# The head of a two-layer decoder step reordered, and the rounding of activations and weights taken in turn with scale and shift

## What is computed

```python
mod = silu(c) @ w_ada[layer] + b_ada[layer]            # 6 x 1024: shift, scale, gate, twice
h = rms_norm(x, norm1) * (1 + sc1) + sh1
y = even_mixer(h, ...)    # layer 0: one input projection (3592 columns), DeltaNet and short convolution
    # layer 1: q, k, v projection (3072 columns), dilated window attention
x = x + g1 * (y @ w_out)
h = rms_norm(x, norm2) * (1 + sc2) + sh2
x = x + g2 * hier_moe(h)  # 32 experts, the two best of the best group for each token
```

## Time and profile before

| | us |
|---|---|
| median of 3 runs | 1290.17 (1289.33 to 1292.78) |
| the profiled execution | 1288.16 |
| its span, first to last instruction | 1286.3 |
| PE busy | 1169.5 (91%) |
| DVE busy | 491.4 (38%) |
| ACT busy | 318.6 (25%) |
| POOL busy | 41.9 (3%) |

### The profile page before, as it was taken

How to read it: one execution, slowest core, us unless ns; L and a number is a source line. 1 busy time by engine, 2 the same in 40 slices (tenths; PEclk the granted TensorE clock), 3 DMA queues, 4 the chain that set the end, 5 groups by cost and what they waited for, 6 DMA issues and landing times.

```text
span 1286.3 us, 18265 instructions
## 1 busy us (share of the span) xinstructions
PE 1169.5 (91%) x7640; PEld 794.1 (62%) x7640; DVE 491.4 (38%) x1228; ACT 318.6 (25%) x600; POOL 41.9 (3%) x85
## 2 busy tenths in 40 slices
PE   3879999989788899999999699998897999999996
PEld 2679878778555655555553599865466455555444
DVE  0267233452323423333333533355425233333334
ACT  0266301020101221111111444454413211111114
POOL 0000000200010000000000200200001000000000
PEclk9679999997779899999999799999997999999998
DMA  9643122396646199999998344599881799999851
GB/s 287 210 141 110 55 66 66 115 336 212 205 153 259 47 402 386 378 380 373 374 377 272 114 135 155 173 319 330 270 343 34 283 419 366 375 363 385 355 202 43
DMA packets 122886, 317.21 MB, mean 247 GB/s; under 512 B 9136, under 2 KB 93136, under 8 KB 96166
## 3 DMA queue, kind: packets, MB, share of 16 engines
q1 hardware_dynamic: 115652, 304.87, 64.3%
q0 software_dynamic: 2336, 7.84, 2.0%
q10 hardware_dynamic: 4802, 3.18, 1.0%
HBM read 309.37 MB, written 6.49 MB: 246 GB/s over the span
## 4 chain that ended last, share of the span: by engine, by line
PE 81%; DVE 12%; ACT 3%; issue 2%; DMA 1%; SPq 1%; ACTq 0%; DVEq 0%
PE bank L1544 17%; PE bank L1105 11%; PE bank L1565 9%; PE bank L1507 5%; PE bank L1582 4%; PE bank L1069 3%; PE bank L1168 3%; PE bank L1071 3%; PE bank L1070 3%; PE bank L1202 3%; PE bank L1160 2%; DVE arena L2001 2%; DVE xT L2007 2%; PE bank L1064 1%; PE bank L1525 1%
## 5 line engine op out<-in xcount | busy, mean ns | idle before, releaser
L1544 PE MATMUL bank<-arena 128*64 128x512 f32 x768 | 225.2, 592 | 0.5 <-DVE gslot L2455 0.5
L1544 PEld LDWEIGHTS bank<-arena 128*64 128x64 f32 x768 | 71.7, 137 | 108.7 <-issue 108.0
L1707 ACT ACTIVATE arena<-bank 128x512 f32<-128x512 f32 (+7 forms) x150 | 76.5, 536 | 206.3 <-PE bank L1071 54.2
L1565 PE MATMUL bank<-ring,scratch 128*64 128x512 f32 x512 | 120.3, 613 | 1.1 <-ACT scratch L1707 1.1
L1544 PE MATMUL bank<-ring,arena 128*64 128x512 f32 x256 | 112.5, 592 | 0.0
L1069 PE MATMUL bank<-hTh,wh 128*128 128x320 f32 x304 | 96.7, 318 | 14.3 <-DVE wl L2066 14.3
L1105 PE MATMUL bank<-hT,ring 128*128 128x320 f32 x352 | 99.6, 440 | 0.6 <-issue 0.6
L1070 PE MATMUL bank<-hTl,wh 128*128 128x320 f32 x304 | 96.1, 316 | 0.0
L1071 PE MATMUL bank<-hTh,wl 128*128 128x320 f32 x304 | 96.0, 316 | 0.0
L2007 DVE SCALAR_TENSOR_TENSOR xT<-bank,mod,xT 128x256 f32<-128x256 f32 x144 | 69.0, 479 | 66.2 <-PE bank L1105 55.7
L2007 DVE SCALAR_TENSOR_TENSOR scratch<-scratch,gslot,bank 128x256 f32<-128x256 f32 x32 | 21.7, 678 | 163.3 <-ACT scratch L1917 163.3
(11 more groups left out here) (309 smaller groups left out, 1746.1 us busy)
## 6 DMA issues: line engine op xcount, KB each, us to landing
ring<-in_w_exp_down_dram SPq DMA_DIRECT2D x64, 1024.0 KB, 8.9
arena<-in_w_exp_gate_dram SPq DMA_DIRECT2D x48, 1024.0 KB, 8.8
arena<-in_w_exp_up_dram SPq DMA_DIRECT2D x48, 1024.0 KB, 10.8
ring<-in_w_ada_dram SPq DMA_DIRECT2D x44, 1024.0 KB, 11.7
ring<-in_w_exp_gate_dram SPq DMA_DIRECT2D x16, 1024.0 KB, 10.8
ring<-in_w_exp_up_dram SPq DMA_DIRECT2D x16, 1024.0 KB, 10.2
ring<-in_w_in_even_dram SPq DMA_DIRECT2D x14, 1024.0 KB, 5.6
ring<-in_w_qkv_odd_dram SPq DMA_DIRECT2D x8, 1024.0 KB, 5.6
```

The source lines that it names most:

```text
L1544: ins = pe.matmul(bank[0][SLOTS * w:SLOTS * w + SLOTS, :].rearrange("p (w f) -> p w f", w=2), hg[:, q % 2, c, s0:s0 + SLOTS], weights[w][: ...
L1565: ins = pe.matmul(bank[2 + d][rows, :], hidT[:, P * f + SLOTS * w:P * f + SLOTS * w + SLOTS], x[:, w, D * f + 512 * d:D * f + 512 * d + 51 ...
L1707: return act.activation(dst, src, ACT.Copy)
```

## The change

In the head the squares go right behind x, DVE adds them up (as it already did for the norms behind the mixers), and PE sums only the last chunk over the partitions. The row of u = 6 and turn 4 stand ahead of the spread. The two weight halves that layer 0 needs first are rounded ahead of hp; ACT then does four hp, and after that one hh and one hp in turn; the third half comes last. In layer 1 half 0 goes ahead of hp, half 1 behind the third hh, half 2 last. DVE follows the same order. POOL multiplies by the token's factor first in layer 0's first norm (into another buffer, `tiny`), by the gain first in the other norms. PE no longer waits in `norm` for hp and hs. The halves 0 to 2 leave the mixers' lists.

```diff
@@ plan_head @@
                     for c in range(C):
                         fills("head", ("x", c), ("dve", ("x", c)))
                         makes("head", "dve", ("x", c))
+                        if c >= 2:
+                            makes("head", "dve", ("acc", "01", c - 1))
+                    makes("head", "dve", ("acc", "01", C - 1))
+                    makes("head", "act", ("squares",))
                 if u == 4:
                     fills("head", ("stats",), ("act", "std01"))
                     makes("head", "act", ("stats",))
                     makes("head", "dve", ("root",))
+                if u == 6:
                     fills("head", ("nbc",), ("dve", ("xn01", C - 1)))
                     makes("head", "dve", ("stats",))
@@ plan_mixer0 @@
-            for n in range(NH):
-                next_half(n)
@@ norm_samples (POOL) @@
-                after(pool, "dve", f"gain{tag}")
-                after(pool, "dve", f"rs{tag}")
-                link(pool.tensor_tensor(hs, xs, of_token, ALU.mult))
-                link(pool.tensor_tensor(hs, hs, gainA[:, :, 1:NCOND].unsqueeze(3).to_broadcast([P, C, NB, LS]), ALU.mult))
+                of_row = gainA[:, :, 1:NCOND].unsqueeze(3).to_broadcast([P, C, NB, LS])
+                if tag == "01":
+                    after(pool, "dve", f"rs{tag}")
+                    part = tiny[:, :].rearrange("p (c b t) -> p c b t", c=C, b=NB)
+                    link(pool.tensor_tensor(part, xs, of_token, ALU.mult))
+                    after(pool, "dve", f"gain{tag}")
+                    link(pool.tensor_tensor(hs, part, of_row, ALU.mult))
+                else:
+                    after(pool, "dve", f"gain{tag}")
+                    link(pool.tensor_tensor(hs, xs, of_row, ALU.mult))
+                    after(pool, "dve", f"rs{tag}")
+                    link(pool.tensor_tensor(hs, hs, of_token, ALU.mult))
@@ norm, head (PE) @@
-                after(pe, "act", (f"hp{tag}", C - 1))
-                after(pe, "pool", f"hs{tag}")
...
                     elif what == "stats":
-                        for c in range(C):
-                            norm_sum("01", c)
+                        after(pe, "dve", ("acc", "01", C - 1))
+                        claim(pe, k)
+                        filled(token_squares(B(k), C - 1, True, True), k)
@@ norm_apply (ACT) @@
+                def shifted(c):
+                    after(act, "dve", (f"xn{tag}", c))
+                    result("act", (f"hp{tag}", c), act.activation(
+                        hT[:, c, 0:NP_], scratch[:, c, 0:NP_], ACT.Identity,
+                        scale=gainA[:, c, 0:1], bias=mod[:, l, j, c, 0:1]))
+                def rounded(c):
+                    after(act, "act", (f"hp{tag}", c))
+                    result("act", ("hh", l, c), copy(hTh[:, c, :], hT[:, c, :]))
+                if j == 3:
+                    for c in range(C):
+                        shifted(c)
+                    return
+                split_half(l, 0)
+                if l == 0:
+                    split_half(l, 1)
+                    after(act, "dve", "gain01")
+                for c in range(4):
+                    shifted(c)
+                after(act, "pool", f"hs{tag}")
+                for c in range(C):
+                    rounded(c)
+                    if c + 4 < C:
+                        shifted(c + 4)
+                    if l == 1 and c == 2:
+                        split_half(l, 1)
+                split_half(l, 2)
@@ accumulate, norm_stats, norm_apply (DVE) @@
+            def accumulate(tag, c):
+                after(dve, "act", (f"sq{tag}", c))
+                if c >= 2:
+                    after(dve, "dve", ("acc", tag, c - 1))
+                result("dve", ("acc", tag, c), add(scratch[:, c, :], scratch[:, c, :], scratch[:, c - 1, :]))
...
                 for c in range(C):
                     result("dve", (f"xn{tag}", c), mul(scratch[:, c, 0:NP_], xT[:, c, 0:NP_], B(k)[:, 0:NP_]))
+                    if tag == "11" and c == 3:
+                        split_half(1, 0)
...
+                    if l == 0:
+                        split_half(0, 0)
+                        split_half(0, 1)
                     for c in range(C):
                         after(dve, "act", ("hh", l, c))
                         result("dve", ("hl", l, c), ...)
+                        if l == 1 and c == 2:
+                            split_half(1, 1)
+                    split_half(l, 2)
```

More of the change, by code:

```diff
@@ L701, in trunk_program @@
         for l in range(2):
-            DVE_ORDER += ["gain11", "root11"] + normed("11") if l else ["gain01"]
-            DVE_ORDER += [("hl", l, c) for c in range(C)]
+            DVE_ORDER += ["gain11", "root11"] + normed("11") if l else ["gain01", ("lo", 0, 0), ("lo", 0, 1)]
+            for c in range(C):
+                DVE_ORDER += [("hl", l, c)] + ([("lo", 1, 1)] if l == 1 and c == 2 else [])
+            DVE_ORDER += [("lo", l, 2)]
             if l == 0:
@@ L714, in trunk_program, with first_chunks @@
         DVE_ORDER += ["rootf"] + [("yt", i) for i in (1, 3, 5)]
+        def first_chunks(l):
+            order = [("hi", l, 0)] + ([("hi", l, 1)] if l == 0 else []) + [(f"hp{l}1", c) for c in range(4)]
+            for c in range(C):
+                order += [("hh", l, c)] + ([(f"hp{l}1", c + 4)] if c + 4 < C else []) + \
+                         ([("hi", l, 1)] if l == 1 and c == 2 else [])
+            return order + [("hi", l, 2)]
         ACT_ORDER = []
         for step in steps_of("head", "act"):
-            ACT_ORDER += [("sq01", c) for c in range(C)] + ["std01"] if step == ("stats",) else [step]
+            ACT_ORDER += [("sq01", c) for c in range(C)] if step == ("squares",) else ["std01"] if step == ("stats",) else [step]
         for l in range(2):
-            ACT_ORDER += (["std11"] if l else []) + [("hp%d1" % l, c) for c in range(C)] + [("hh", l, c) for c in range(C)]
+            ACT_ORDER += (["std11"] if l else []) + first_chunks(l)
             if l == 0:
@@ L1113, in token_squares @@
                 return ins
[L1115 to L1123, removed]
             def project_out(l, rhs):
@@ L1736, in norm_apply @@
                         hT[:, c, 0:NP_], scratch[:, c, 0:NP_], ACT.Identity,
-                        scale=gainA[:, c, 0:1], bias=mod[:, int(tag[0]), j, c, 0:1]))
-                if tag[1:] == "1":
-                    l = int(tag[0])
-                    after(act, "pool", f"hs{tag}")
-                    for c in range(C):
-                        after(act, "act", (f"hp{tag}", c))
-                        result("act", ("hh", l, c), copy(hTh[:, c, :], hT[:, c, :]))
+                        scale=gainA[:, c, 0:1], bias=mod[:, l, j, c, 0:1]))
[3 more added lines that the diff above has]
+                if j == 3:
+                    for c in range(C):
+                        shifted(c)
[7 more added lines that the diff above has]
+                after(act, "pool", f"hs{tag}")
+                for c in range(C):
+                    rounded(c)
[4 more added lines that the diff above has]
+                split_half(l, 2)
             def split_half(l, n):
@@ L1962, in _ @@
                     result("act", ("cond",), act.activation(condT[:, :, 0:NCOND], cols[:, :, 17:26], ACT.Silu))
+                elif what == "squares":
+                    act.wait_ge(ld_const, 16)
+                    norm_squares("01")
                 elif what == "stats":
-                    norm_stats("01")
+                    norm_std("01")
                 else:
@@ L2292, in mixer1 @@
             def mixer1():
-                for n in range(24):
+                for n in range(NH, 24):
                     split_half(1, n)
@@ L2525, in _ @@
                     continue
+                if what == "acc":
+                    accumulate(*i)
+                    continue
                 if what == "stats":
```

35 lines of the change are left out of this document (14 added, 21 removed).

## The result

The changed kernel took 1270.62 us (median of 4 runs, 1267.41 to 1273.02) beside 1290.8 for the kernel before on the same chip (4 runs, 1289.33 to 1292.78): ratio 0.9841, 95% interval 0.9811 to 0.9871. The profiled execution took 1272.55, its span is 1270.8 instead of 1286.3.

A forecast was written before the change was run, and what follows sets the result against it. TensorE makes up four fifths of the chain and idles in the head and both layers' rounding. Layer 0's 16.2 us (head included) plus layer 1's 3.1 give 19.3: 1288.16 becomes 1268.9, median about 1271, range 1265 to 1279.

The forecast's parts named there:

- The head: From the start to layer 0's first hp: hp starts at 51.1 instead of 63.80, a gain of 12.7 us.
- row6: Head, TensorE's adaLN pair of units 6 and 7: moved ahead of the spread, takes 1.86 us, no wait for weights.
- The collision: Layer 0 rounding: VectorE's lo and GpSimd's steps take turns on the SBUF port, 4.5 us from hp's start to first hh.
- the first rival: No port collision: 2.15 us come back in layer 0 and 1.15 in layer 1, total 1267.6 us; chance 0.20.
- The first chunk: Layer 0's first projection chunk: starts on the first hl with a cold clock, ends 6.8 us after the first hh.
- T: Moment of the first hh in layer 0, forecast at 55.6 us, 4.5 us after hp's start.
- Layer 1: Layer 1's norm and rounding: second projection chunk at 740.3 instead of 743.4, gain 3.1 us, bounds 1.3 and 4.3.
- At nothing: Edits priced at zero: TensorE's removed waits for all hp and hs, and the swapped multiplications before the routers.
- its own test: Prediction wrong as a whole if layer 0's stretch from second chunk to output projection grows by more than 3 us.
- The second rival: Lower clock in row6, layer 0's second chunk and layer 1 takes back 5.6 us: gain 13.7, 1276.5 us; chance 0.20.
- The third: Rival in the head: row6 waits for its weights and starts 10.5 us later, gain 8.8, 1281.4 us; chance 0.04.
- the fourth: Rival in layer 0: chunks starting in pieces keep the clock down beyond the second; all 14 give 1320 us; chance 0.04.

The follow-up runs named there:

- after: First profile of the changed kernel, against the kernel before: profiled execution 1272.55 us, median 1270.62 us, ratio 0.9841.
- head_only: Changed kernel with its new head but the rounding order of the kernel before: 1278.58 us, ratio 0.9901; repeated 1277.8 us, ratio 0.9901.
- before: The only profile of the kernel without the change: profiled execution 1288.16 us; median 1290.8 us beside the changed kernel.
- round_only: Changed kernel with the old head (all eight chunks summed on TensorE, old row order) and the new rounding: 1286.49 us, ratio 0.996.
- whole_again: The changed kernel measured and profiled once more with no edit: 1268.69 us, ratio 0.9831 against the kernel before.
- whole_third: The unedited changed kernel, a third profile, measured beside the version with TensorE's waits put back: 1266.73 us, ratio 0.9833.
- halves_apart: Changed kernel with layer 0's second lo behind the third hl and layer 1's weight halves reordered: 1268.14 us, ratio 0.9826; repeated 1264.38 us, ratio 0.9811.

## Why the prediction was right, and where it was off

The forecast of 1271 lies 0.4 from the median of 1270.62, and that close a hit is partly luck: later runs of the same kernel have medians of 1268.69 and 1266.73, and inside the sum a head that gained more than forecast stands against a first chunk and a layer 1 that gained less.

**The head**, forecast 12.7: 14.24 in after. The sums ended 0.5 sooner than forecast (42.87, less 0.39 for the later x): the six records took 0.79, not the 1.25 priced from sums that had run at the lower clock, at which head_only's six take 1.29. The spread ran at the higher level too, 1.05 instead of the 1.84 of the earlier trace rows, another 0.8. Squares and additions were hidden, row6 did not wait for its weights and took 1.93, both as said. The window in which the earlier trace rows had TensorE stand still is filled in after, at a granted clock of 0.96:

```profile
40.00:44.00 4.00, 4.00 (x58) 2.81 (x54) 0.41 (x3) 0.99 (x3) 0.00 (x0) 0.96 1.09 344
```

**The collision.** 4.5 was forecast from hp to the first hh; it is 4.21 (49.95 to 54.16), and head_only, with no lo beside the steps, shows the two at 1.08. So the first rival's mechanism is out, though its time, 1267.6, lies among the medians of the later runs. The rule cited in the prediction (the Trainium skill, "SBUF — State Buffer", "Who interferes with whom") holds here in numbers: lo 0, multiply, lo 1, add, one after the other, 3.25 from the start of the first lo to the end of the second, for two lo of about 1.2 each.

**The first chunk.** Forecast at T + 6.8 it was evicted at T + 7.57 (54.16 to 61.73), the one term of layer 0 that was too small: TensorE's matmuls came back to 2.4 GHz only at 60.9, so 20 of the chunk's 24 ran at the lower level (15 before), and it took 6.48 from its first matmul where it had taken 5.66. The second chunk took 3.46, as said. In all 17.4 from the last copy of x to the second eviction (44.19 to 26.75), for 16.2.

**Layer 1.** 3.1 forecast, 2.5 measured (23.65 to 21.13). The spread came 3.91 behind the deviation instead of 3.22, for which no row names a reason (3.93 in head_only, so it isn't the order of rounding), and what follows hs took 11.4 instead of 11.1; the two last steps, 3.29 with lo between, were 0.3 cheaper than priced. The term also held the clock's dip of the earlier trace rows, 1.8 us, which is in before and not in after (granted clock 1.00 from 717 to 728). That dip isn't bound to the order of rounding: round_only has one, and head_only, with the old order, has none. Its two chunks, behind a first matmul at 727.89:

```profile
731.68 0.44 ACT L1710 ACTIVATE arena<-bank 128x320 f32<-128x320 f32 x1 [3.29 <-PE bank L1085]
...
735.20 0.44 ACT L1710 ACTIVATE arena<-bank 128x320 f32<-128x320 f32 x1 [0.70 <-PE bank L1085]
```

Against head_only's 22.81, at the same clock and with the same late spread, the new order brings 1.7 to 1.8 us; the forecast's 3.1 counted the end of the dip as a gain of the order, and its lower bound of 1.3 was nearer.

**At nothing.** The swapped multiplications cost nothing: GpSimd ended at 405.52, its reader began at 409.73 (as the earlier trace rows).

```profile
404.44 1.08 POOL L993 TENSOR_TENSOR hT<-hT,mod 128x512 f32<-128x512 f32 x1
...
409.73 1.06 PE L1463 MATMUL bank<-hT,wr 128*36 128x64 f32 x16
```

The removed waits were wrongly reasoned. "hl waits for the same work" holds for the last hl, not for the first, on which the chunk starts: with the waits back the first matmul is 2.48 later. The sum was not touched, since I had let the chunk start on its first hl; but that start is bought by the removal.

**What was carried to the end.** The forecast let the gain of layer 0 pass through whole. By its own test (not over 3 us between the second chunk and the output projection) the first profile fails, 293.87 for 290.66; whole_again and whole_third pass, 290.33 and 290.32. It is the clock at 338 to 349 us: the transposes take 7.14 in 5 of the 13 profiles of changed kernels and 4.08 or 4.84 in the others, and in either form in executions of one program, so it is not a fixed cost of the change; how often the kernel before has it, its one profile (4.85) can't say. In whole_third the parts add up near the forecast: 17.3 + 2.7, with 0.2 from the rest, 20.1 for 19.3.

**The second rival** priced the lower clock at 5.6. Its head happened, in head_only and halves_apart, in 2 of the 11 profiles with this order of the head, and cost 5.3 us (16.85 for 11.5), not the 1.7 of row6 alone, since row4, the turns and the spread were at the lower level too. Its long second chunk never came, 3.46 in every one. It was set up as a way for the change to go; it is something that varies between executions of one program. The third and the fourth did not occur.

## What to carry to other kernels

When a chain crosses engines, look for a link that is done for all items although another engine could take part of it or the next needs only the first: here the eight-fold sums on TensorE, and the rounding of all activations and weights ahead of the first matmul. Before an edit is priced by one profile, profile the same program twice and cut both at the same marks: columns that repeat belong to the program; a column that does not (here by up to 5 us, mostly with TensorE's rows at one clock level or the other) is no price of an edit. And price a VectorE instruction with two SBUF operands beside a GpSimd one as in series, as here lo beside hs, or move it where GpSimd is done.

## What the hardware showed that I had not expected

The level of TensorE's clock in the head differs between executions of the same instructions: 1.2 GHz from 27.5 or 29.8 us to past the gain in halves_apart and head_only, 2.4 GHz again from within row4 in most others, 5.3 us apart. In the three profiles where it was low soonest (27.3 to 27.5 us), TensorE had waited 2.08 to 2.24 us for weights at 25 us; in head_only, where it stayed low, 1.39 us, in the seven where it came back, 0.99 to 1.56. With that pause filled by four matmuls the fall came where these seven have it (30.9 and 31.9, for 29.4 to 32.4), with eight at 34.2, the transposes of x being 3 us later too. What sets the level stays open. The two places that vary most, head and transposes, are worth 5.3 and 3.5 us; the runs of the changed kernel spread over 7.1 (1265.88 to 1273.02, 15 runs). That the places make the spread is argued from the profiles: most single runs have no trace.
